# Expert passes of 96 slots in place of 128 in a two-layer hybrid decoder trunk on one core

## The reference

```python
def swiglu(h, w_gu, w_down):
    g, u = jnp.split(h @ w_gu, 2, axis=-1)
    return (jax.nn.silu(g) * u) @ w_down

def moe_swiglu(h, router_w, w_gu, w_down):
    logits = jnp.einsum('bsd,de->bse', h, router_w, ...)
    top_v, top_i = lax.top_k(logits, EXPERT_TOPK)          # 2 of 8
    probs = jax.nn.softmax(top_v, axis=-1)
    gate = jnp.einsum('bsk,bske->bse', probs, one_hot(top_i, N_EXPERTS))
    y = jnp.zeros_like(h)
    for e in range(N_EXPERTS):
        y = y + gate[..., e:e + 1] * swiglu(h, w_gu[e], w_down[e])
    return y
```

## Time and profile before

| | before |
|---|---|
| median of 3 runs | 1342.3 us |
| profiled execution, first to last instruction (span) | 1341.0 us |
| what the median has over that span | 1.3 us |
| TensorE busy, share of the span | 98% |
| token mixers and dense layer, up to the first expert matmul | 578.3 us |
| the eight expert items | 578.3 to 1333 us |
| last scatter and the end | 1333 to 1341 us |
| one item in the middle | 94.0 us |

### The profile page before, as it was taken

How to read it: one execution, slowest core, us unless ns; L and a number is a source line. 1 busy time by engine, 2 the same in 40 slices (tenths; PEclk the granted TensorE clock), 3 DMA queues, 4 the chain that set the end, 5 groups by cost and what they waited for, 6 DMA issues and landing times.

```text
span 1341.0 us, 17732 instructions
## 1 busy us (share of the span) xinstructions
PE 1320.5 (98%) x6332; PEld 1089.3 (81%) x6332; DVE 1034.0 (77%) x963; ACT 911.9 (68%) x996; POOL 87.8 (7%) x67
## 2 busy tenths in 40 slices
PE   9999999999999999999999999999999999999997
PEld 7867888888898777888888888888888888888885
DVE  5886675544467866689898898898898998988984
ACT  6688745444366877467687787686776876876873
POOL 0420000000012200000000000000010000000000
PEclk9999999999999999999999999999999999999999
DMA  8634456554466334889999999999999999999992
GB/s 289 201 95 150 154 170 217 189 188 157 147 197 214 95 127 157 302 311 396 341 377 390 377 381 391 369 382 388 370 382 385 366 389 365 382 390 368 382 391 51
DMA packets 172905, 381.22 MB, mean 284 GB/s; under 512 B 9098, under 2 KB 29236, under 8 KB 172852
## 3 DMA queue, kind: packets, MB, share of 16 engines
q1 hardware_dynamic: 169904, 370.01, 76.6%
q0 software_dynamic: 2304, 8.39, 2.4%
q10 hardware_dynamic: 644, 2.12, 0.4%
HBM read 374.20 MB, written 6.29 MB: 284 GB/s over the span
## 4 chain that ended last, share of the span: by engine, by line
PE 93%; ACT 3%; DVE 3%; issue 1%; DMA 1%; DVEq 0%; POOLq 0%; ACTq 0%
PE ps L1130 18%; PE ps L1132 18%; PE ps L1131 18%; PE ps L702 11%; PE ps L704 10%; PE ps L703 10%; PE ps L1196 1%; ACT w_hi L1314 1%; PE ps L834 1%; ACT mix L1304 1%; PE ps L827 1%; PE ps L887 1%; DVE mix L1736 1%; PE ps L1211 1%; DVE mix L1733 1%
## 5 line engine op out<-in xcount | busy, mean ns | idle before, releaser
L1965 DVE TENSOR_TENSOR w_lo<-mix,w_hi 128x2048 fp32r<-128x2048 f32 (+1 forms) x192 | 408.1, 2149 | 67.4 <-ACT w_hi L1549 65.8
L1549 ACT CAST w_hi<-mix 128x2048 fp32r<-128x2048 f32 (+1 forms) x190 | 340.7, 1810 | 85.5 <-PE ps L1132 85.5
L1698 DVE TENSOR_TENSOR w_lo<-raw,w_hi 128x2048 fp32r<-128x2048 f32 (+3 forms) x93 | 197.2, 2126 | 108.5 <-ACT w_hi L1314 107.8
L1130 PE MATMUL ps<-w_hi,eT_hi 128*128 128x512 f32 x704 | 279.0, 396 | 0.0
L1132 PE MATMUL ps<-w_hi,eT_lo 128*128 128x512 f32 x704 | 274.4, 390 | 0.0
L1131 PE MATMUL ps<-w_lo,eT_hi 128*128 128x512 f32 x704 | 274.4, 390 | 0.0
L1314 ACT CAST w_hi<-raw 128x2048 fp32r<-128x2048 f32 (+3 forms) x93 | 165.5, 1783 | 119.3 <-PE ps L704 107.2
L1965 DVE TENSOR_TENSOR w_lo<-raw,w_hi 128x2048 fp32r<-128x2048 f32 (+1 forms) x96 | 193.2, 2032 | 17.0 <-ACT w_hi L1549 16.1
L1549 ACT CAST w_hi<-raw 128x2048 fp32r<-128x2048 f32 (+1 forms) x96 | 163.4, 1713 | 48.0 <-PE ps L1132 44.4
L702 PE MATMUL ps<-w_hi,hT_hi 128*128 128x512 f32 (+1 forms) x464 | 179.7, 387 | 1.5 <-DVE w_lo L1978 0.9
L704 PE MATMUL ps<-w_hi,hT_lo 128*128 128x512 f32 (+1 forms) x464 | 176.5, 380 | 0.0
(11 more groups left out here) (207 smaller groups left out, 1487.0 us busy)
## 6 DMA issues: line engine op xcount, KB each, us to landing
mix<-in_expert_w_gate_up_dram SPq DMA_DIRECT2D x111, 1024.0 KB, 10.1
raw<-in_expert_w_gate_up_dram SPq DMA_DIRECT2D x49, 1024.0 KB, 8.5
mix<-in_expert_w_down_dram SPq DMA_DIRECT2D x48, 1024.0 KB, 11.0
raw<-in_w_in_dram SPq DMA_DIRECT2D x28, 1024.0 KB, 5.3
raw<-in_expert_w_down_dram SPq DMA_DIRECT2D x24, 1024.0 KB, 12.5
raw<-in_dense_w_gate_up_dram SPq DMA_DIRECT2D x20, 1024.0 KB, 5.1
mix<-in_expert_w_down_dram SPq DMA_DIRECT2D x25, 512.0 KB, 7.7
raw<-in_dense_w_down_dram SPq DMA_DIRECT2D x9, 1024.0 KB, 4.9
```

The lines of the kernel that those rows point to most:

```text
L1130: pe.matmul(out_, l_hi, w_hi[q][:, cols], start=first, stop=False, skip_group_check=True)
L1549: act.copy(w_hi[q][:, 0:m], e_raw[raw_of(p, first)][:, 0:m]).then_inc(e_hi_ready, 1)
L1698: dve.tensor_tensor(w_lo[q][:, 0:m], raw[u % RAW][:, 0:m], w_hi[q][:, 0:m].bitcast(F32), ALU.subtract).then_inc(split, 1)
L1965: dve.tensor_tensor(w_lo[q][:, 0:m], e_raw[raw_][:, 0:m], w_hi[q][:, 0:m].bitcast(F32), ALU.subtract).then_inc(e_split, 1)
```

## The change

`CAP` becomes 96, so `PASSES` becomes 3 (the second and third run only where an expert has more than 96 tokens), and the third pass starts at slot 160 in place of 192, with the gates of the slots that the second pass had set to 0. Every tile of an item with a slot dimension shrinks to 96: the stationary operands `eT` and `e_hidT` have 96 columns; gate, up and down products, silu, hidden, result and gathered rows have 96 partitions; the transpositions take 96 partitions and a 96 x 96 identity; the copies behind them have 96 columns a block. The moving side of the large matmuls, the loads, the casts and the splits stay as they are. On DVE the gates and slots of the later passes are made after the low part of unit 3 and not before the one-hot. The loads of a third pass are added to SP's program and its fetches and scatters to POOL's.

```diff
-CAP = 128
+CAP = 96
 PASSES = -(-T // CAP)
+SLOT0 = tuple(min(k * CAP, T - CAP) for k in range(PASSES))
...
-        e_act = mix[:, o:o + 512]
+        e_act = mix[0:CAP, o:o + 512]
...
-        x_rows, y_rows = h[:, 0, :], h[:, 1, :]
+        x_rows, y_rows = h[0:CAP, 0, :], h[0:CAP, 1, :]
...
-                        last = three_e(ps[piece // 2][:, 0:w], [part_[:, kt, :] for part_ in eT], q,
+                        last = three_e(ps[piece // 2][0:CAP, 0:w], [part_[:, kt, :] for part_ in eT], q,
                                        slice(kk * w, (kk + 1) * w), kt == 0, kt == DT - 1)
...
-                            last = three_e(ps[4 + half][:, :], [part_[:, b, :] for part_ in e_hidT], split_of(p, first),
+                            last = three_e(ps[4 + half][0:CAP, :], [part_[:, b, :] for part_ in e_hidT], split_of(p, first),
...
-                    last = pe.transpose(ps[2][:, b * P:(b + 1) * P], e_hid[:, b * P:(b + 1) * P], ident)
+                    last = pe.transpose(ps[2][:, b * CAP:(b + 1) * CAP], e_hid[:, b * P:(b + 1) * P], ident[0:CAP, 0:CAP])
...
-                    last = pe.matmul(ps[3][:, 0:2], sel[:, t, :], stage[:, 2 + 2 * t:4 + 2 * t], start=t == 0, stop=t == NT - 1)
+                    last = pe.matmul(ps[3][0:CAP, 0:2], sel[:, t, :], stage[:, 2 + 2 * t:4 + 2 * t], start=t == 0, stop=t == NT - 1)
...
                         last = pe.transpose(ps[6 + g][:, m * CAP:(m + 1) * CAP], x_rows[:, (4 * g + m) * P:(4 * g + m + 1) * P],
-                                            ident)
+                                            ident[0:CAP, 0:CAP])
...
-                act.activation(e_act[:, 0:FF_W[j]], ps[0][:, 0:FF_W[j]], ACT.Silu).then_inc(e_silu, 1)
+                act.activation(e_act[:, 0:FF_W[j]], ps[0][0:CAP, 0:FF_W[j]], ACT.Silu).then_inc(e_silu, 1)
...
-                    act.mul(y_rows[:, half * 512:(half + 1) * 512], ps[4 + half][:, :], gate_now).then_inc(y_out, 1)
+                    act.mul(y_rows[:, half * 512:(half + 1) * 512], ps[4 + half][0:CAP, :], gate_now).then_inc(y_out, 1)
...
-                dve.tensor_tensor(e_hid[:, 0:w], e_act[:, 0:w], ps[1][:, 0:w], ALU.mult).then_inc(hid_done, 1)
+                dve.tensor_tensor(e_hid[:, 0:w], e_act[:, 0:w], ps[1][0:CAP, 0:w], ALU.mult).then_inc(hid_done, 1)
...
-            for k in range(PASSES):
+            def gates_of(k):
+
                 at = 1 + k * NEXP
-                if k:
-                    dve.scalar_tensor_tensor(out=route[:, 0:2, at:at + NEXP], in0=sign, scalar=float(-k * CAP), in1=others,
-                                             op0=ALU.add, op1=ALU.add)
                 for t in range(NT):
                     last = dve.tensor_copy(route[:, 3 + 2 * t, at:at + NEXP], ex[:, t, :])
-            step(last)
+                return last
+
+            def slots_of(k):
+
+                at = 1 + k * NEXP
+                return dve.scalar_tensor_tensor(out=route[:, 0:2, at:at + NEXP], in0=sign, scalar=float(-SLOT0[k]), in1=others,
+                                                op0=ALU.add, op1=ALU.add)
+
+            step(gates_of(0))
             one_hot(1, 1)
             split_low_e(0, 3, True)
+            for k in range(1, PASSES - 1):
+                slots_of(k)
+                gates_of(k)
+            k = PASSES - 1
+            at = 1 + k * NEXP
+            step(slots_of(k))
+            for t in range(NT):
+                last = dve.scalar_tensor_tensor(out=route[:, 3 + 2 * t, at:at + NEXP], in0=route[:, t, at:at + NEXP],
+                                                scalar=float(k * CAP - SLOT0[k]) - 0.5, in1=ex[:, t, :], op0=ALU.is_gt, op1=ALU.mult)
+            step(last)
             item(0, True)
```

More of the change, by code:

```diff
@@ L400, in trunk @@
         o = part(512)
-        e_act = mix[:, o:o + 512]
+        e_act = mix[0:CAP, o:o + 512]
         o = part(512)
-        e_hid = mix[:, o:o + 512]
+        e_hid = mix[0:CAP, o:o + 512]
         e_hidT = [over(f"e_hidT_{n}", [P, 4, CAP], mix_at + 4 * part(4 * CAP)) for n in ("hi", "lo")]
@@ L410, in trunk @@
         stage = mix[:, o:o + 6]
-        gate_next, gate_now = mix[:, o + 7:o + 8], mix[:, o + 8:o + 9]
+        gate_next, gate_now = mix[0:CAP, o + 7:o + 8], mix[0:CAP, o + 8:o + 9]
         o = part(16 * 5)
@@ L1151, in gate_up_e @@
                         for kt in range(lo, hi):
-                            last = three_e(ps[0][:, :], [part_[:, kt, :] for part_ in eT], q,
+                            last = three_e(ps[0][0:CAP, :], [part_[:, kt, :] for part_ in eT], q,
                                            slice((kt - lo) * 2 * w, (kt - lo + 1) * 2 * w), kt == 0, kt == DT - 1)
@@ L1185, in down_last @@
                             at = (b - lo) * D + half * 512
-                            last = three_e(ps[4 + half][:, :], [part_[:, b, :] for part_ in e_hidT], split_of(p, False),
+                            last = three_e(ps[4 + half][0:CAP, :], [part_[:, b, :] for part_ in e_hidT], split_of(p, False),
                                            slice(at, at + 512), False, b == BLOCKS[-1] - 1)
@@ L1254, in finish_items @@
                             at = (b - lo) * D + half * 512
-                            last = three_e(ps[4 + half][:, :], [part_[:, b, :] for part_ in e_hidT],
+                            last = three_e(ps[4 + half][0:CAP, :], [part_[:, b, :] for part_ in e_hidT],
                                            split_of(piece, False), slice(at, at + 512), False, b == BLOCKS[-1] - 1)
@@ L1616, in silu_last @@
                 act.wait_ge(hid_done, i * FF - 1)
-                act.activation(e_act[:, 0:FF_W[-1]], ps[0][:, 0:FF_W[-1]], ACT.Silu).then_inc(e_silu, 1)
+                act.activation(e_act[:, 0:FF_W[-1]], ps[0][0:CAP, 0:FF_W[-1]], ACT.Silu).then_inc(e_silu, 1)
             def turned_high_e(no, blocks):
@@ L2072, in places_next @@
                 dve.wait_ge(meta_done, no)
-                dve.tensor_copy(rows_next[:, :], ps[3][:, 0:1])
-                dve.tensor_copy(gate_next, ps[3][:, 1:2]).then_inc(meta_next, 1)
+                dve.tensor_copy(rows_next[:, :], ps[3][0:CAP, 0:1])
+                dve.tensor_copy(gate_next, ps[3][0:CAP, 1:2]).then_inc(meta_next, 1)
             def one_hot(column, n_staged):
@@ L2111, in hidden_last @@
                 w = FF_W[-1]
-                dve.tensor_tensor(e_hid[:, 0:w], e_act[:, 0:w], ps[0][:, w:2 * w], ALU.mult).then_inc(hid_done, 1)
+                dve.tensor_tensor(e_hid[:, 0:w], e_act[:, 0:w], ps[0][0:CAP, w:2 * w], ALU.mult).then_inc(hid_done, 1)
             def turned_low_e(no, blocks):
```

## The result

The changed kernel took 1346.6 us (median of 8 runs, 1345.9 to 1349.2), the kernel before 1343.6 in the same comparison. The ratio is 1.0022, interval 1.0013 to 1.0032: a little slower, where 1332.9 us and a gain of 9.4 us had been forecast. The profiled execution has a span of 1344.1 us against 1341.0.

What follows compares the result with a forecast made beforehand. PE was taken to set the pace of the items. Savings of 6.4 + 0.8 + 1.3 + 0.1 + 0.2 + 0.15 + 0.5 = 9.4 us gave a span of 1331.6 and a time of 1332.9 us; 8-in-10 range 1328 to 1339.5.

Steps and rivals of the forecast that it cites:

- What bounds the kernel: Items: PE, busy all 94.0 us of one, sets the pace; ACT, DVE and the loads follow.
- The large matmuls: 3168 matmuls, 396 an item: spacing of 0.227 us unchanged by 96 stationary columns, 0 gained; bounds nothing or 10.5 us gained.
- the 13 ns: Large matmuls' spacing: what remains beyond 0.42 ns per moving column, the same at 288 and 512 moving columns.
- The last rival: Large matmuls: the load of 96 columns takes a slower path; 3.0 ns more spacing eats all the gain; 4%.
- The second rival: Large matmuls: spacing shrinks with the load, 10.5 us more off, 1322.4 us; 12%.
- Transpositions: Turns and turn_rows: 240 transpositions with 96 moving columns for 128 save 27 ns each, 6.4 us.
- places: Four instructions an item with 2 moving columns: shorter float32 loads save 0.027 us in each of 36; taken as 0.8 us.
- exposed loads: First matmul behind each turn, six places an item: its unhidden load is 27 ns shorter, 1.3 us.
- The end: Behind the last turn: copies give 0.15 us, the last scatter of 96 rows for 128 gives 0.5 us.
- Queues: SP, POOL and DMA queues: no new executed SP instruction, loads have 12 us to spare; 0.
- First item: DVE's queue around unit 3's low part: 0.1 us gained there, 0.2 before the first item, nothing late.
- The sum: Whole kernel: all terms take 9.4 us off the span, 1341.0 to 1331.6 us; median 1332.9.

Runs made afterwards that it cites:

- the first experiment: The changed kernel with 96 slots, but the large matmuls' stationary tiles keep 128 columns, the last 32 zeros: 1334.4 us, ratio 0.993 to the kernel before.
- the 88 rows above: The changed kernel with 88 slots in place of 96 and 128 stationary columns kept for the large matmuls: 1332.9 us, ratio 0.9928 to the kernel before.

## Why the prediction was wrong

**What bounds the kernel**: right. PE held 93% of the chain before and after, and no wait came in.

**The large matmuls**: wrong, and this step alone turned the sign. I took 0 "because the 13 ns are the same at 288 and 512 columns, where the load had 133 and 227 ns to hide in". That shows that the load's length is hidden at a given placement; it doesn't show that nothing else of the load matters. What the stream of rows 5 had, and I didn't look at, was a stationary block that is level with its moving block modulo 256 bytes and 128 columns wide. The runs put in its place: 96 columns cost 2.7 ns a matmul and packing them at 384 bytes 1.5 ns more, 4.2 ns together, 3168 x 4.2 = 13.3 us. That the place of the blocks sets the spacing is shown in the kernel by shifts alone; why 96 columns at the old place cost 2.7 ns is open. The last rival named the place and the price from which it decides (3.0 ns), at a chance of 4%, but with another mechanism, a slow load, which the bf16 and float32r loads rule out. The second rival, spacing that shrinks with the load, fell too for these matmuls; at 256 moving columns, which the items don't have, it is what the streams show.

**Transpositions, places and exposed loads**: right. 27 ns a transposition was measured as 27, and the first experiment, which has these terms without the exposed loads, gives 94.04 - 93.02 = 1.02 us an item where 240 and 36 instructions of the forecast come to 0.9. The exposed loads are 0.03 us shorter each (0.29 for 0.32).

**The end**: the last scatter, before and after:

```profile
1337.71 1.44 POOL L2255 DMA_INDIRECT out_dram<-h_scaled,rows_now  x1 [46.95 <-ACT h_scaled L1629]
1343.23 0.19 ACT L1679 COPY mix<-mix 128x2 f32<-128x2 f32 x1 [6.31 <-DMA out_dram<-h_scaled,rows_now]
```

5.5 us for 6.1: 0.6 gained, 0.5 forecast. The reason given, a time by the row, isn't borne out: the 88 rows above took 6.3. **Queues**: right, a 1 MB load of the same group lands in 12.2 us against 12.5. **First item**: DVE's queue moved as worked out, and the trace names no wait of PE there.

**The sum**: 9.4 us forecast, and 1341.0 - 1331.7 = 9.3 in the version that keeps the stationary operand. That it is so close is partly luck: this version lacks the exposed loads' 1.3 us, so the forecast for it is 8.1; its items give 0.12 us more each than forecast, and its first expert matmul starts 0.5 us earlier, at 577.77, where 0.3 was forecast for the two ends of the first item. Adding 3168 x 4.2 ns = 13.3 and taking off the exposed loads' 1.3 gives 1343.7, where the changed kernel's span is 1344.1. The range excluded it because "for 8 in 10" left out the only case with this sign; a form that no row of the trace showed deserved more than 4%, with 3168 instances behind it and 3 ns as its break-even.

## What to carry to other kernels

A float32r matmul with 512 moving columns isn't cheaper with fewer stationary ones and can be dearer; what shrank here is what has the small size on its moving side (the transpositions), the exposed loads of `places` and behind turns, and the copies. When such a tile shrinks, keep the stationary blocks' pitch and width and their distance to the moving blocks, and leave the spare columns zero: it gave 9.4 us here. With 256 moving columns measure anew, as narrower streams were faster there. In a kernel bound by thousands of equal matmuls, compare their spacing first of all, to the nanosecond, also after a change that moves only addresses.

## What the runs showed of the hardware

- The spacing of float32r matmuls with 512 moving columns depends on the distance of the stationary and the moving block in SBUF, with a period of 256 bytes: with 128 stationary columns 226.7 ns at best and up to 234.2, with no other engine at work. The Trainium skill (TensorE: Matmul & The Clock Gate, Step-by-step: what each phase is for) says that loading the next weights takes no SBUF read bandwidth from the running matmul, as there are two read ports. That the distance counts all the same suggests that the two reads meet somewhere; this is an inference, and where they would meet was not shown.
- It also depends on the width, without order: 226.8 at 124 columns, 233.3 at 120, 230.0 at 96. With 256 moving columns it falls with the width: 120.0, 115.8 and 113.5 ns at 128, 96 and 64.
- Some forms have two spacings and keep for a whole stream the one that the stream ahead led them to (226.7 or 231.7 for 96 columns 128 bytes off; 229.0 or 233.4 for 112 columns). What is remembered stays open.
- Why 96 columns at distance 0 settle at 230 and 128 at 227 wasn't settled either, nor was it tried whether another distance suits 96 columns better inside the kernel.
